# Decode attention: five of eight key pages multiplied by the query on GpSimd, summed on VectorE

## The chip, the cores and the metric

One NeuronCore of one Trainium2 chip. The metric is the device time of one execution in microseconds. All data is float32.

## The reference

One inference step of a two-layer decoder with 256 prompt tokens and 8 sample sequences of one new token each. Layer 0 is a gated MLP over positions and a mixture of experts (MoE). Then one shared key/value pair is projected. Layer 1 is block-sparse attention and a second MoE. The change lies in the attention of the 8 sample tokens. Each of these sequences has 1024 past positions, kept in 8 pages of 128 positions, which a page table scatters over a pool:

```
rows = pool[page_table]                      # keys, values: (8, 1024, 8 heads, 128)
gate = einsum('hqd,nhd->hqn', q, k_mean)     # query times the mean key of each block of 256
_, sel = top_k(gate, 3)                      # 3 of the 4 past blocks, and the own block
s = einsum('hqd,hqjkd->hqjk', q, k_g) * HEAD_DIM ** -0.5
p = softmax(concat([s, s_own]))
o = einsum('hqjk,hqjkd->hqd', p, v_g) + p_own @ v_own
```

## The kernel before

The program is written engine by engine, with semaphores by hand; each engine runs its own list in order. Keys, values and weights go through a ring of 8 slots in SBUF, filled by SyncE (SP). A page is 128 positions on 128 partitions, 1024 elements (8 heads of 128) in each; a slot holds four pages. One sequence's keys are 4 MB in 8 DMAs and its values the same. K(s) goes to slots 2-3 or 4-5, V(s) to 0-1 or 6-7, in turn. SP's order is K0, V0, K1, V1, ..., K7, V7, then the output weights and the second MoE's. K(s) waits until the scores of sequence s-2 are done (`s_made`), V(s) until the value products of s-2 are (`pv_out`); K2 waits for the V projection.

The attention loop has steps s = 0 to 8. In step s, VectorE makes the scores of sequence s and, between their pages, the softmax of sequence s-1 and the causal softmax of one prompt head (two in step 7). Scores (`keys`, L1514): TensorE spreads the query of sequence s over all partitions with matmuls against the identity (`queries`, L1119), heads 0-3 in bank 6, heads 4-7 in bank 7. VectorE runs one fused multiply and sum per page and head (L1525): key tile from SBUF times query from PSUM, summed to one score column, with the product written over the keys. It goes twice over the 8 pages, first for half 0 (heads 0-3), then for half 1. After fixed pages it does the other work:

- half 0, page 0: `blocks` (L1545), which drops the block of least score sum: L1548 to L1559, all in a chain; L1551, L1552, L1554 and the two L1557 read two SBUF operands. Page 1: `prompt_max` (L1534). Page 2: `maxima` (L1561). Page 4: `shift` (L1566, with L1570 and L1571). Page 5: `prompt_norm` (L1575, with L1578 and L1579). Page 6: `row_sums` (L1583).
- half 1, page 0: `denominators` (L1588, with L1592). Page 6: `result` (L1594).

TensorE, in step s: the prompt's logits, the transposed block maxima (L1194), their spread (L1196), the prompt's transposes, the denominator (L1203), 32 value matmuls of sequence s-1 (L1212), the prompt's values, the selection (L1221), the queries of s+1 for half 0 (`next_queries`, which waits for half 0's scores), and with the end of step s the block sums of s (L1171) and the queries of s+1 for half 1 (`open_step`). In step 0 TensorE also does the V projection (L1078), and ScalarE the copies of it (L698 to L706). ScalarE's own loop (L709) has the exponentials and the copies of PSUM banks. GpSimd has nothing in this loop: before it, it stores the k and v rows and clears a pad (L538 to L548), behind it stands the second MoE.

Of the kernel before, what the change touches and what calls it, by code (L numbers as in the profile page):

```python
# [25 lines left out]
P = 128  # L26
D = 1024
# [105 lines left out]
def program(nc, a, o):  # L133

    ctx = ExitStack()
    with ctx:
# [116 lines left out]
        dg = region(11000, H)  # L253
        hm = region(11008, 1)
        yr = region(2112, 3, D)

# [85 lines left out]
        def pair_of(name):  # L342
# [13 lines left out]

        gb_made, gcol_out, gcol_made, gD_out, sD_made, hD_made, yD_out, yD_added = (pair_of(n) for n in [
            "gb_made", "gcol_out", "gcol_made", "gD_out", "sD_made", "hD_made", "yD_out", "yD_added"])
        vecD = pair_of("vector_steps_all")
# [8 lines left out]
            "ps_out", "ps_max", "ps_exp", "ps_norm", "pT_out", "pT_made", "po_out", "po_kept"])  # L368

        qb_out, s_made, gs_out, pm_made, pm_turned, dg_made, mb_out, sc_made, se_made, rs_made, den_out = (  # L370
            sem(n) for n in ["qb_out", "s_made", "gs_out", "pm_made", "pm_turned", "dg_made", "mb_out",
# [119 lines left out]
        def _(pool):  # L491
# [45 lines left out]
            nc.gpsimd.wait_ge(rows_kept, 6)  # L537
            for rows, kname in ((krows, "k"), (vrows, "v")):  # L538
                if kname == "v":
                    pool.wait_ge(v_rows_kept, 2 * H)  # L540
                s_ = k_stored if kname == "k" else stored
                pool.dma_start(o[kname + "_prompt"][0].rearrange("(t p) h d -> p t (h d)", p=P),
                               rows[:, 0:2, :]).then_inc(s_, 16)
                pool.dma_start(o[kname + "_sample"].rearrange("b s h d -> (b s) (h d)"),
                               rows[0:NS, 2, :]).then_inc(s_, 16)
                if kname == "k":
                    pool.wait_ge(k_stored, 32)
                    nc.gpsimd.memset(pe4, 0.0).then_inc(pad_set, 1)  # L548
            moe(1)
# [3 lines left out]
        def _(act):  # L553
# [147 lines left out]
            def keep_v_rows(h):  # L701
                act.wait_ge(v_rows_out, h + 1)
                nc.scalar.activation(vrows[:, 0:2, h * HD:(h + 1) * HD],
                                     PB[2][:, 0:2 * P].rearrange("p (t d) -> p t d", t=2), ACT.Copy)\
                    .then_inc(v_rows_kept, 1)
                nc.scalar.activation(vrows[0:NS, 2, h * HD:(h + 1) * HD], PB[2][0:NS, 2 * P:3 * P], ACT.Copy)\  # L706
                    .then_inc(v_rows_kept, 1)
            act.wait_ge(pad_set, 1)
            for s in range(NS + 1):  # L709
# [21 lines left out]
                for h in V_HEADS[s]:  # L731
# [3 lines left out]
                    if h == H - 1:  # L735
                        keep_v_rows(h)
            act.wait_ge(stored, 64)
            square_and_root(3, sqM, wo_added, 0)
# [521 lines left out]
        def _(dve):  # L1260
# [253 lines left out]
            def keys(s, half, g):  # L1514

                c = s % 2
                k_slot = K_SLOT[s] + g // 4
                if g == 0:
                    dve.wait_ge(qb_out, 2 * s + half + 1)
                if g % 4 == 0 and half == 0:  # L1520
                    arrived(dve, f"K{s}", k_slot, each=64)
                for i in range(4):
                    h = 4 * half + i
                    kb = W[:, k_slot, (g % 4) * D + h * HD:(g % 4) * D + (h + 1) * HD]
                    last = v.tensor_tensor_reduce(kb, kb, PB[6 + half][:, i * P:(i + 1) * P], 1.0, 0.0,  # L1525
                                                  ALU.mult, ALU.add, sc[:, c, g, h:h + 1])
                if g == NPAGE - 1:
                    last.then_inc(s_made, 1)
# [123 lines left out]
```

## Time and profile before

| what | value |
|---|---|
| median of 3 runs | 1179.06 us |
| lowest, highest | 1178.21, 1182.37 us |
| span of the profiled execution | 1183.5 us |
| TensorE, VectorE, ScalarE, GpSimd busy | 90%, 34%, 12%, 3% |
| moved by DMA | 320.68 MB, 271 GB/s on average |
| chain that ended last | PE 82%, DVE 10% |

The profile gives the profiled execution's own time as its span, 1183.5 us. It counts from the first recorded instruction to the last, and it lies 4.4 us above the median of the timed runs. The page and the trace call TensorE PE, VectorE DVE, ScalarE ACT, GpSimd POOL and SyncE SP. A wait is given in brackets behind the instruction that ended it, with the releaser. A line number is that of the kernel.

### The profile page before, as it was taken

The page shows a single profiled execution, that of the slowest core. Times are in us where ns is not written, and L with a number is a line of the kernel's source. Part 1 is how long each engine was busy: PE and PEld are TensorE (multiplying, and loading weights), DVE is VectorE, ACT ScalarE, POOL GpSimd, SP SyncE. Part 2 cuts the span into 40 slices and gives each one's busy share as a digit, 9 for nine tenths or more (in the row PEclk, how much of TensorE's full clock was granted, in tenths as well). Part 3 has the DMA queues.
Part 4 walks back from the last instruction along what each step waited for, and adds up shares of the span by engine and source line. Part 5 has one row for each costly group of instructions (what it writes and reads, how often), then busy time and mean ns, then how long its engine had stood idle before and what let it go on. Part 6 is the DMA issues. An engine that isn't in the chain of part 4 may idle for free.

```text
span 1183.5 us, 14135 instructions
## 1 busy us (share of the span) xinstructions
PE 1068.1 (90%) x5078; PEld 686.2 (58%) x5078; DVE 408.0 (34%) x1753; ACT 145.3 (12%) x322; POOL 35.8 (3%) x56
## 2 busy tenths in 40 slices
PE   6599999989999999998999957574989999999997
PEld 4488889965455555445776734233765455554444
DVE  2034440031112121204676699987031122112113
ACT  1001001021000000002121211111121000000001
POOL 0100000010000000000000000000010000000000
PEclk9799999999999999998999967777998999999999
DMA  9802536054868998889234499999731858988881
GB/s 378 302 9 72 178 127 284 1 226 173 320 248 356 383 400 354 353 348 416 116 142 179 158 353 408 408 408 416 305 143 65 356 212 366 417 355 355 351 350 50
DMA packets 57999, 320.68 MB, mean 271 GB/s; under 512 B 6186, under 2 KB 7594, under 8 KB 47306
## 3 DMA queue, kind: packets, MB, share of 16 engines
q1 hardware_dynamic: 52880, 312.56, 66.1%
q0 software_dynamic: 1424, 5.37, 1.3%
q10 hardware_dynamic: 3634, 1.98, 0.6%
q8 instruction: 33, 0.54, 0.2%
q14 instruction: 28, 0.23, 0.1%
HBM read 315.53 MB, written 4.36 MB: 270 GB/s over the span
## 4 chain that ended last, share of the span: by engine, by line
PE 82%; DVE 10%; ACTq 3%; issue 2%; DMA 1%; SPq 1%; ACT 1%; DVEq 0%
PE bank L1013 19%; PE bank L927 11%; PE bank L1041 10%; PE bank L818 8%; PE bank L994 6%; PE bank L862 5%; PE bank L1097 5%; DVE ring L1525 4%; PE bank L1212 3%; PE bank L1250 3%; PE bank L1078 2%; PE bank L755 2%; PE bank L813 1%; DMA ring<-in_cache_k 1%; PE bank L765 1%
## 5 line engine op out<-in xcount | busy, mean ns | idle before, releaser
L1013 PE MATMUL bank<-ring,arena 128*64 128x512 f32 x1024 | 225.9, 600 | 3.2 <-DVE arena L1405 3.2
L1013 PEld LDWEIGHTS bank<-ring,arena 128*64 128x64 f32 x1024 | 76.2, 138 | 149.1 <-issue 145.6
L927 PE MATMUL bank<-arena 128*128 128x128 f32 (+1 forms) x768 | 136.6, 308 | 1.9 <-DVE xT L1454 1.9
L818 PE MATMUL bank<-arena,ring 128*128 128x264 f32 x512 | 123.4, 400 | 16.0 <-ACT arena L597 13.0
L927 PEld LDWEIGHTS bank<-arena 128*128 128x128 f32 (+1 forms) x768 | 105.1, 189 | 33.8 <-issue 5.0
L818 PEld LDWEIGHTS bank<-arena,ring 128*128 128x128 f32 x512 | 99.1, 197 | 34.4 <-ACT arena L597 13.4
L1041 PE MATMUL bank<-ring,arena 128*64 128x512 f32 x512 | 113.4, 595 | 0.3 <-issue 0.3
L1525 DVE CUSTOM_DVE_ANT_0 ring<-ring,bank 128x128 f32<-128x128 f32 x512 | 111.4, 282 | 5.2 <-DMA ring<-in_cache_k 2.2
L1460 DVE TENSOR_TENSOR arena<-arena,bank 128x512 f32<-128x512 f32 x16 | 11.0, 688 | 214.3 <-PE bank L1013 214.3
L1041 PEld LDWEIGHTS bank<-ring,arena 128*64 128x64 f32 x512 | 36.2, 137 | 63.9 <-issue 63.6
L994 PEld LDWEIGHTS bank<-arena 128*128 128x128 f32 x256 | 63.4, 333 | 15.7 <-issue 11.4
L994 PE MATMUL bank<-arena 128*128 128x264 f32 x256 | 70.3, 420 | 1.7 <-ACT arena L644 1.7
L1097 PE MATMUL bank<-arena,ring 128*128 128x264 f32 x256 | 62.8, 401 | 3.0 <-DVE arena L1279 3.0
L862 PE MATMUL bank<-arena,ring 128*128 128x264 f32 x256 | 63.5, 408 | 0.0
L862 PEld LDWEIGHTS bank<-arena,ring 128*128 128x128 f32 x256 | 61.7, 334 | 2.2 <-DVE xT L1343 2.2
L1454 DVE TENSOR_TENSOR xT<-xT,bank 128x264 f32<-128x264 f32 x128 | 55.0, 429 | 13.0 <-PE bank L994 7.8
L1405 DVE COPY arena<-bank 128x512 f32<-128x512 f32 x16 | 11.1, 692 | 137.0 <-PE bank L927 137.0
L1097 PEld LDWEIGHTS bank<-arena,ring 128*128 128x128 f32 x256 | 49.4, 197 | 14.0 <-DVE arena L1279 3.4
L1212 PE MATMUL bank<-ring,arena 128*32 128x512 f32 x256 | 43.2, 835 | 0.0
L1473 DVE COPY arena<-bank 128x512 f32<-128x512 f32 x16 | 11.1, 692 | 90.1 <-PE bank L1041 90.1
L1525 DVE DVE_READ_ACCUMULATOR2_ANT arena<- 128x1 f32 x512 | 41.8, 82 | 0.0
L1492 DVE RECIPROCAL arena<-arena 128x264 f32<-128x264 f32 x16 | 28.8, 1803 | 24.9 <-ACT arena L670 24.9
(205 smaller groups left out, 856.2 us busy)
## 6 DMA issues: line engine op xcount, KB each, us to landing
ring<-in_moe_w_gate SPq DMA_DIRECT2D x32, 2048.0 KB, 16.8
ring<-in_moe_w_up SPq DMA_DIRECT2D x32, 2048.0 KB, 14.7
ring<-in_moe_w_down SPq DMA_DIRECT2D x32, 2048.0 KB, 12.5
ring<-in_cache_k SPq DMA_DIRECT2D x64, 512.0 KB, 7.5
ring<-in_cache_v SPq DMA_DIRECT2D x64, 512.0 KB, 6.0
ring<-in_a_w_in SPq DMA_DIRECT2D x8, 2048.0 KB, 26.2
ring<-in_a_w_out SPq DMA_DIRECT2D x4, 2048.0 KB, 8.0
ring<-in_w_kv SPq DMA_DIRECT2D x4, 2048.0 KB, 24.1
```

The source lines that it names most:

```text
L818: return mm(bank[:, 0:T], slot(base + k // 2, 2)[:, k % 2, j * P:(j + 1) * P], hT[:, k, :], start=(k == 0), stop=(k == KT - 1))
L862: last = mm(PB[j % 2][:, 0:T], slot(c // 4, 4)[:, c % 4, j:D:KT], vT[:, c, :], start=(c == 0), stop=(c == CT - 1))
L927: last = mm(PB[k // 4][:, (k % 4) * P:(k % 4 + 1) * P], hr[0:n, t, k * P:(k + 1) * P], hot[0:n, t, :, :].rearrange("p e s -> p (e s)"), st ...
L994: last = mm(y_bank(i, j)[:, 0:T], dr[:, j:D:KT], sT, start=True, stop=True)
L1013: last = mm(bank[64 * e:64 * e + 64, :], hg[:, k, CAP * e:CAP * (e + 1)], slot(base + e, KT)[:, k, :], start=(k == 0), stop=(k == KT - 1))
L1041: last = mm(PB[4 + half][64 * e:64 * e + 64, :], heT[:, f, CAP * e:CAP * (e + 1)], slot(down[0] + e, FT)[:, f, 512 * half:512 * (half + 1) ...
L1097: last = mm(acc(g)[:, 0:T], w, h[:, k, :], start=(k == 0), stop=(k == KT - 1))
L1212: last = mm(PB[4][32 * q:32 * q + 32, :], pe4[:, c, g, :], W[:, v_slot + g // 4, (g % 4) * D + 512 * half:(g % 4) * D + 512 * (half + 1)], ...
L1250: last = mm(PB[j % 2][:, 0:T], slot(W_O + h // 4, 4)[:, h % 4, j:D:KT], aT[:, h, :], start=(h == 0), stop=(h == H - 1))
L1454: v.tensor_tensor(xT[:, j, :], xT[:, j, :], y_bank(i, j)[:, 0:T], ALU.add).then_inc(moe_done if isinstance(i, int) and i == NPAIR - 1 else ...
L1492: link(v.reciprocal(rsh, rmh))
L1525: last = v.tensor_tensor_reduce(kb, kb, PB[6 + half][:, i * P:(i + 1) * P], 1.0, 0.0, ALU.mult, ALU.add, sc[:, c, g, h:h + 1])
```

## The change

For sequences 1 to 7, pages 1, 2, 4, 5 and 7 are multiplied on GpSimd, a whole page of 1024 elements for all heads at once, in place. VectorE sums each such page over 128 elements for 8 heads with one reduction in half 1. Pages 0, 3 and 6 stay as they were, and sequence 0 too. As GpSimd reads its query from SBUF, ScalarE copies the two banks into a new tile `qrow`, of two buffers. `qrow` lies where the normed input of the K and V projections lay, so the first copy waits for the V projection to end. VectorE's first page of a half waits for the copy instead of the matmuls. The first half's `s_made` is given after page 6. The stores of the rows are written as a function, and four pairs of semaphore names in the MoE are shared by two forms of it of which one runs.

```
+        qrow = region(0, 2, D)
+        BY_POOL = (1, 2, 4, 5, 7)
...
-        gb_made, gcol_out, gcol_made, gD_out, sD_made, hD_made, yD_out, yD_added = (pair_of(n) for n in [
-            "gb_made", "gcol_out", "gcol_made", "gD_out", "sD_made", "hD_made", "yD_out", "yD_added"])
+        sD_made, hD_made, yD_out, yD_added = silu_made, he_made, y_out, y_added
+        gcol_out, gcol_made, gD_out, gb_made = sT_out, sT_made, heT_out, heT_made
...
+        q_kept, k_by_pool = sem("q_kept"), sem("k_by_pool")
...
+            store_rows(krows, "k", k_stored)
+            pool.wait_ge(k_stored, 32)
+            nc.gpsimd.memset(pe4, 0.0).then_inc(pad_set, 1)
+            pool.wait_ge(v_rows_kept, 2 * H)
+            store_rows(vrows, "v", stored)
+            for s in range(1, NS):
+                pool.wait_ge(q_kept, 2 * s)
+                for g in BY_POOL:
+                    arrived(pool, f"K{s}", K_SLOT[s] + g // 4, each=64)
+                    kb = W[:, K_SLOT[s] + g // 4, (g % 4) * D:(g % 4 + 1) * D]
+                    nc.gpsimd.tensor_tensor(kb, kb, qrow[:, s % 2, :], ALU.mult).then_inc(k_by_pool, 1)
             moe(1)
...
+            def keep_q(s, half):
+
+                act.wait_ge(qb_out, 2 * s + half + 1)
+                if s == 1 and half == 0:
+                    act.wait_ge(vp_out, H)
+                nc.scalar.activation(qrow[:, s % 2, 512 * half:512 * (half + 1)], PB[6 + half][:, :], ACT.Copy)\
+                    .then_inc(q_kept, 1)
...
+                if s + 1 < NS:
+                    keep_q(s + 1, 0)
+                    keep_q(s + 1, 1)
             act.wait_ge(stored, 64)
...
+                by_pool = s >= 1 and g in BY_POOL
                 if g == 0:
-                    dve.wait_ge(qb_out, 2 * s + half + 1)
-                if g % 4 == 0 and half == 0:
+                    if s == 0:
+                        dve.wait_ge(qb_out, half + 1)
+                    else:
+                        dve.wait_ge(q_kept, 2 * (s - 1) + half + 1)
+                if half == 0 and g % 4 == 0:
                     arrived(dve, f"K{s}", k_slot, each=64)
...
+                if by_pool and half == 1:
+                    dve.wait_ge(k_by_pool, (s - 1) * len(BY_POOL) + BY_POOL.index(g) + 1)
+                    last = v.tensor_reduce(sc[:, c, g, :], W[:, k_slot, (g % 4) * D:(g % 4 + 1) * D]
+                                           .rearrange("p (h d) -> p h d", h=H), AX.X, ALU.add)
+                elif not by_pool:
+                    for i in range(4):
+                        h = 4 * half + i
+                        kb = W[:, k_slot, (g % 4) * D + h * HD:(g % 4) * D + (h + 1) * HD]
+                        last = v.tensor_tensor_reduce(kb, kb, PB[6 + half][:, i * P:(i + 1) * P], 1.0, 0.0,
+                                                      ALU.mult, ALU.add, sc[:, c, g, h:h + 1])
+                if g == (6 if s >= 1 and half == 0 else NPAGE - 1):
                     last.then_inc(s_made, 1)
```

## Rows read from the trace of the kernel before

**Rows 1.** The page's 40 slices of 29.6 us: busy tenths of VectorE and DMA engines.
```profile
DVE  2034440031112121204676699987031122112113
...
DMA  9802536054868998889234499999731858988881
```

**Rows 2.** Windows: length, busy us by engine, granted TensorE clock, DMA share, GB/s.
```profile
720.45:740.90 20.45, 12.78 (x74) 7.00 (x74) 18.69 (x154) 2.72 (x8) 0.00 (x0) 0.75 1.03 407
820.00:825.00 5.00, 2.52 (x9) 1.91 (x9) 3.35 (x26) 0.88 (x2) 0.00 (x0) 0.61 1.02 433
```

**Rows 3.** The chain of waits around the keys of sequence 7: start, us, what.
```profile
788.04 12.11 DMA ring<-in_cache_k
```

**Rows 4.** VectorE's timeline: ends of sequence 1's, 6's and 7's scores, start of 7's.
```profile
695.74 0.08 DVE L1525 DVE_READ_ACCUMULATOR2_ANT arena<- 128x1 f32 x1
...
798.19 0.08 DVE L1525 DVE_READ_ACCUMULATOR2_ANT arena<- 128x1 f32 x1
800.29 0.29 DVE L1525 CUSTOM_DVE_ANT_0 ring<-ring,bank 128x128 f32<-128x128 f32 x1 [2.03 <-DMA ring<-in_cache_k]
...
821.96 0.08 DVE L1525 DVE_READ_ACCUMULATOR2_ANT arena<- 128x1 f32 x1
```

**Rows 5.** VectorE's timeline in one step, which begins at 736.74.
```profile
736.66 0.08 DVE L1525 DVE_READ_ACCUMULATOR2_ANT arena<- 128x1 f32 x1
...
737.17 0.28 DVE L1525 CUSTOM_DVE_ANT_0 ring<-ring,bank 128x128 f32<-128x128 f32 x1
...
737.38 0.28 DVE L1525 CUSTOM_DVE_ANT_0 ring<-ring,bank 128x128 f32<-128x128 f32 x1
...
740.92 0.29 DVE L1539 TENSOR_REDUCE arena<-arena 128x1 f32<-128x128 f32 x1
741.13 0.41 DVE L1540 TENSOR_REDUCE arena<-arena 128x1 f32<-128x256 f32 x1
...
746.31 0.29 DVE L1578 TENSOR_SCALAR arena<-arena 128x128 f32<-128x128 f32 x1
746.51 0.35 DVE L1579 TENSOR_SCALAR arena<-arena 128x256 f32<-128x256 f32 x1
...
747.89 0.25 DVE L1585 TENSOR_REDUCE arena<-arena 128x8 f32<-128x64 f32 x1
...
756.22 0.17 DVE L1596 TENSOR_TENSOR arena<-arena,bank 128x8 f32<-128x8 f32 x1 [0.90 <-PE bank L1221]
```

**Rows 6.** Groups of GpSimd's products by shape: busy us, mean ns, idle before.
```profile
L516 POOL TENSOR_TENSOR arena<-arena,roots 128x264 f32<-128x264 f32 x16 | 11.3, 736 | 289.0 <-DVE roots L1275 289.0
...
L499 POOL TENSOR_TENSOR wr<-arena,gains 128x128 f32<-128x128 f32 x2 | 0.8, 403 | 0.0
...
L499 POOL TENSOR_TENSOR wr<-arena,gains 128x32 f32<-128x32 f32 x2 | 0.5, 243 | 2.3 <-DMA arena<-in_moe_w_re 2.3
```

**Rows 7.** Timelines of ScalarE and TensorE: a 128x512 copy, a half's query matmuls.
```profile
734.01 0.60 ACT L725 ACTIVATE arena<-bank 128x512 f32<-128x512 f32 x1 [6.07 <-PE bank L1212]
...
737.07 1.11 PE L1122 MATMUL bank<-consts,arena 128*128 128x128 f32 x8
```

**Rows 8.** Timelines in the second MoE, where GpSimd multiplies from 879.07 to 884.72.
```profile
880.49 0.73 POOL L516 TENSOR_TENSOR arena<-arena,roots 128x264 f32<-128x264 f32 x1
...
879.93 0.20 DVE L1353 TENSOR_TENSOR arena<-bank,rbias 128x40 f32<-128x40 f32 x1 [0.41 <-PE bank L895]
...
880.64 0.61 DVE L1367 TENSOR_TENSOR arena<-arena,consts 128x12 f32<-128x12 f32 x1
...
881.98 0.67 DVE L1371 TENSOR_TENSOR arena<-arena 128x12 f32<-128x12 f32 x1
...
883.43 0.20 DVE L1377 TENSOR_REDUCE arena<-arena 128x12 f32<-128x48 f32 x1
```

**Rows 9.** Step 1: ScalarE's last copy of V rows, GpSimd's last row store.
```profile
678.62 0.25 ACT L706 ACTIVATE arena<-bank 8x128 f32<-8x128 f32 x1
...
679.92 0.52 POOL L544 DMA_DIRECT2D out_v_sample<-arena  x1
```

More of the change, by code:

```diff
@@ L537, in _, with store_rows @@
             nc.gpsimd.wait_ge(rows_kept, 6)
[L538 to L541, printed above, removed]
+            def store_rows(rows, kname, done):
                 pool.dma_start(o[kname + "_prompt"][0].rearrange("(t p) h d -> p t (h d)", p=P),
-                               rows[:, 0:2, :]).then_inc(s_, 16)
+                               rows[:, 0:2, :]).then_inc(done, 16)
                 pool.dma_start(o[kname + "_sample"].rearrange("b s h d -> (b s) (h d)"),
[L545 to L548, printed above, removed]
+                               rows[0:NS, 2, :]).then_inc(done, 16)
+            store_rows(krows, "k", k_stored)
[9 more added lines that the diff above has]
+                    nc.gpsimd.tensor_tensor(kb, kb, qrow[:, s % 2, :], ALU.mult).then_inc(k_by_pool, 1)
             moe(1)
@@ L1517, in keys @@
                 k_slot = K_SLOT[s] + g // 4
+                by_pool = s >= 1 and g in BY_POOL
                 if g == 0:
-                    dve.wait_ge(qb_out, 2 * s + half + 1)
-                if g % 4 == 0 and half == 0:
-                    arrived(dve, f"K{s}", k_slot, each=64)
[L1522 to L1527, printed above, removed]
+                    if s == 0:
[3 more added lines that the diff above has]
+                if half == 0 and g % 4 == 0:
+                    arrived(dve, f"K{s}", k_slot, each=64)
+                if by_pool and half == 1:
[9 more added lines that the diff above has]
+                if g == (6 if s >= 1 and half == 0 else NPAGE - 1):
                     last.then_inc(s_made, 1)
```

## The prediction

> **What bounds the kernel now.** I read the slices of the page first. In the decode-attention stage, about 697 to 822 us, VectorE shows 9, 9, 9, 8, 7 tenths and the DMA engines 9 throughout [rows 1]. So two resources are full side by side, and the question is which lets go last. The windows say it more finely: a stretch of 20.45 us holds 18.69 us of VectorE instructions and no GpSimd work, at a DMA share of 1.03 and 407 GB/s [rows 2]. One step moves the keys and values of one sequence: 16 pages of 0.524 MB, 8.39 MB; at 0.408 MB per us that is 20.5 us, the step's own length. In the chain of waits the keys' DMA ends a piece of 12.11 us at 800.15 [rows 3], and VectorE starts sequence 7 at 800.29 after 2.03 us of waiting for it [rows 4]. VectorE paces the stage up to there by a hair, the transfer paces its last step. Behind the last score at 822.04 [rows 4] comes a fixed sequence of round trips, the output projection and the second MoE, which move 1:1 with it.
>
> In a step, 64 fused products at a pitch of 0.21 us (737.17 to 737.38 [rows 5]) are 13.3 us; the small instructions and one wait are the other 7.1 us. The change attacks the 13.3 us, but the transfer stays 20.5 us a step. That caps what it can bring: an earlier VectorE waits for K7 at 800.29, and only the 21.75 us from there to 822.04 can shrink.
>
> **VectorE, added and removed.** In sequences 1 to 7, 40 of 64 products go: 40 x 0.208 = 8.3 us. Five sums over 128x1024 come. The trace has none; reductions of 128 and 256 elements take 0.29 and 0.41 us [rows 5], so 0.96 ns an element and 0.41 + 768 x 0.96 ns = 1.15 us, 1.06 us as pitch (an instruction begins 0.08 us before the end printed for the one before). Bounds: 0.98 us (1024 x 0.96 ns) and 1.64 us (four times the 256 row). I take 1.06: five are 5.3 us, net 3.0 us less per step. But cover goes too. From the row sums' start to the result lie 8.33 us (747.89 to 756.22, with a wait of 0.90 for TensorE [rows 5]): denominator, 32 value matmuls, a copy, a selection, none of them shortened. VectorE would then have 0.17+0.83+0.50+2.12+0.83+2.12+0.83 = 7.4 us in it and wait 0.9 us, as now. Undisturbed, a step is 7.85 us to its row sums (today 747.89 - 736.74 = 11.15, less 16 products), 8.33, and 1.14 for result and last sum: 17.3 us. Under the transfer's 20.5, so that would decide.
>
> **GpSimd.** 35 products of 128x1024, both operands in SBUF. Rows: 128x32 0.243 us, 128x128 0.403 us, 128x264 0.735 us [rows 6]. First to third, the slope is 0.492 us/232 = 2.12 ns an element: 2.35 us, 2.31 as pitch. Low end 1.9 us (the slope between the first two, 1.67 ns), high end 2.85 us (the 264 row in proportion). I take 2.31, since that row alone has two full operands. Five are 11.6 us, below a step, so GpSimd is not itself the bound. It starts once both halves of the query are in SBUF: the last score of a step ends at 736.74 [rows 5], the four query matmuls' end at 738.18, ScalarE's 128x512 copy takes 0.60 us [rows 7]. That is 2.2 us into the step; the products end at 4.5, 6.8, 9.1, 11.5 and 13.8. The 14 copies on ScalarE are 8.4 us on an engine busy 2.72 of 20.45 us [rows 2]; behind them it next waits for maxima, so they cost nothing outside step 1. If GpSimd's queue were late, behind it stands only the second MoE's first work.
>
> **Two engines in one another's way.** The trace already shows GpSimd and VectorE meeting. While GpSimd multiplies 128x264 at a pitch of 0.70 us (one starts at 880.49, so the next at 881.19), VectorE's L1367, 12 elements with two SBUF operands, starts at 880.64 and takes 0.61 us, to 881.25; L1371 starts at 881.98 and takes 0.67 us, to 882.65, where product ends fall at 881.89 and 882.59. A reduction in between takes 0.20 us, and an add with a PSUM operand 0.20 us [rows 8]. So: a VectorE instruction with two SBUF operands is held to the end of the running GpSimd product; one with a single SBUF operand is not, which frees the key products (their query is in PSUM) and the sums. The Trainium skill, SBUF — State Buffer, section Who interferes with whom, states that rule: the pair excludes each other for the whole instruction. The trace agrees, with 0.61 us for what takes 0.17. The same section counts a two-port fp32 tensor_scalar among the held; no row here has one beside GpSimd, and by it case 2 below (1187) would fall away.
>
> Two SBUF operands have, in a step: L1551, L1552, L1554 and twice L1557 (block choice), L1570 and L1571 (shift), L1592. L1578 and L1579 have one, but 128 elements more cost them 0.06 us [rows 5], 2.1 elements a ns against the reductions' 1.04: they must use a second way in. I count them held; unheld is case 2. An instruction issued unlinked behind a held one (L1571, L1557's second) I let slip through with it; that it loses another 2.3 us is case 3. An ordinary step, from its last score: the block choice reaches L1557 at 2.3, just as GpSimd starts, and ends at 2.8. Causal maxima 1.3, block maxima 0.6, page 3 0.83, the add before L1570 0.2: 5.6. L1570 held to 6.9, L1578 to 9.2, L1579 to 11.6. Page 6; row sums at 12.5. Result at 20.8, last page's sum done at 21.96. Today 798.27 - 695.84 = 102.43 us for five steps [rows 4], 20.49 each. 5 x 1.47 = +7.4 us.
>
> **Step 1.** VectorE now waits there for the copied query, and ScalarE makes it only after its last V rows (678.87 [rows 9]): halves at 679.5 and 680.1. Today page 0 and the block choice are done earlier, in the shadow of the V projection. They now stand behind 679.5 and meet GpSimd at once, whose row stores leave it at 680.44 [rows 9]: products end at 682.8, 685.1, 687.4, 689.7, 692.1. L1551, L1552, L1554, L1557 are held to the first, second, third, fourth. Row sums at 695.4, the step ends at 704.9; today it ended at 695.84 [rows 4], with row sums 9.3 us before, 686.6. +9.0 us.
>
> **The queue of SP.** V2 waits for the values of sequence 0, so it starts 8.8 us later and K3 and all pages with it. K7 lands at 809.1 instead of 800.3, and is wanted at 704.9 + 109.8 = 814.7: hidden. **Step 7** has two heads: 1.4 us more, 23.4 us, against 822.04 - 798.27 = 23.8 with its wait. -0.4. Sum: 9.0 + 7.4 - 0.4 = +16.0 us on the profiled execution's 1183.5 us. That execution is 4.4 us (0.4%) above the median of the runs; the difference is carried over whole: 1179.1 + 16.0 = 1195.1.
>
> The other edits cost nothing: semaphore names shared by two forms of the MoE of which one runs; row stores in the old order on the old queue; the first half's semaphore at page 6, which frees the query's bank sooner.
>
> **The rivals.** (1) Not slower: the holds don't bite, say because GpSimd's reads of wide tiles leave gaps. Then 17.3 us of work stand in 20.5 us of transfer. Row sums of step 1 come 0.8 us later (687.4), K7 too; the last step takes 17.3 + 1.4 = 18.7 us instead of 21.75: -2.2, 1176.9. It decides from the point where a step's holds are below 3 us. Against it: [rows 8]. 0.17. With pages at the 433 GB/s of 820 to 825 us [rows 2], 99 us of transfer would be 5.7 us shorter still: 1171; nothing says pages get that. 0.06. (2) L1578 and L1579 not held: steps of 18.7 us, so the transfer decides, 8.8 us late: 8.8 + 20.95 - 21.75 = +8.0, 1187. 0.17. (3) Every unlinked second instruction is held again, and the tiny L1543 and L1564: steps of 25.3 us, step 1 +11.3, step 7 26.7: 11.3 + 24.2 + 2.9 = +38, 1217. 0.12. The forecast runs from +5 (products of 1.9 us) to +32 (2.85 us), 1184 to 1211; sums of 1.64 us would add about 14. 0.48.
>
> **The numbers.** 1195 us. The range 1177 to 1211 takes in case 2 and the forecast and touches case 1. A measurement of this kernel tells 0.5%, 6 us, from no change: faster 0.06, same 0.20 (case 1 and the low edge of the forecast), slower 0.74.
>
> **What would show it.** Right: five GpSimd products of about 2.3 us a step; L1570 and L1578 of 1 to 2 us instead of 0.17 and 0.29; L1551 to L1557 long in step 1 alone; steps near 22 us; DMA share below 1 from step 3 on; sequence 1's first key product at 679.5. Wrong: L1578 still 0.29 us (case 2); steps of 20.5 us with VectorE waiting for keys (case 1); a page's sum far from 1.15 us; GpSimd products above 3.4 us, since then 2.2 + 5 x 3.4 + 1.1 = 20.3 us and GpSimd itself is the bound; key products longer than 0.28 us.

## The result, and the profile after

| what | before | after |
|---|---|---|
| median, lowest to highest, us | 1179.02, 1178.21 to 1182.37 | 1232.59, 1231.50 to 1240.36 |
| span of the profiled execution, us | 1183.5 | 1229.8 |
| VectorE, GpSimd busy | 34%, 3% | 37%, 9% |

The changed kernel is slower: ratio 1.0456, 95% interval 1.0418 to 1.0494, +53.6 us. The forecast was 1195 us; the measured time lies above the range's high end of 1211 us. The direction and the kind of cause were right; which instructions pay, and so the size, was not.

The two profiled executions don't start the attention stage at the same time: the first key product of sequence 0 is at 651.69 us before and at 645.64 us after, so the difference of the spans (46.3 us) understates what the stage lost. A profiled execution's span lies 1.7 us under its time here (1229.8 and 1231.50 us), so that of before took some 1185 us, about 6 us above the median, and its stage begins 6.05 us later. Below, the stage is measured from that product to the first instruction of the last block choice: 171.58 us before, 223.09 us after, +51.5 us. That is nearly all of the loss.

The 40 slices of the page (30.7 us each), as [rows 1]: busy tenths of VectorE and the DMA engines.

```profile
DVE  2024440040111210146665999999304012121013
DMA  9702544067698888894345588888903769888881
```

In slices 24 to 28 (707 to 861 us) VectorE shows 9 as before, but the DMA engines no longer do: 8 instead of 9. One step of the stage, from the end of sequence 1's scores at 702.70 to that of sequence 2's, in the columns of [rows 2]:

```profile
702.70:729.95 27.25, 13.60 (x74) 7.15 (x74) 24.81 (x80) 3.93 (x11) 11.54 (x5) 0.69 0.84 311
```

The step takes 27.25 us where [rows 2] had 20.45. VectorE has 80 instructions instead of 154 and is nevertheless busy for 24.81 us instead of 18.69. The transfer ran at 407 GB/s there and runs at 311 here, share 0.84 instead of 1.03: it now waits for VectorE, since the ring's slots come free later (the share is 1.00 and more up to 723 us, and 0.01 from 724 to 726). GpSimd works 11.54 us. From sequence 1's end on the step hardly varies: from one block choice to the next the seven steps take 29.72, 27.23, 27.27, 27.37, 27.26, 27.28 and 28.43 us, where they took 28.29, 20.45, 20.47, 20.47, 20.68, 22.39 and 22.14 before.

Where it goes is in the timelines of this step, GpSimd's first and then VectorE's. The line numbers have moved: L1580, L1581, L1583 and L1586 are the L1551, L1552, L1554 and L1557 of before, L1572 is L1543, L1593 is L1564, L1599 and L1600 are L1570 and L1571, L1607 and L1608 are L1578 and L1579, L1614 the row sums (L1585), L1625 the result (L1596), L1554 the fused product (L1525), which is not the L1554 of before, now L1583. An `x5` in a timeline row is five instructions without a gap, and its second number is their whole length.

```profile
704.86 11.54 POOL L558 TENSOR_TENSOR ring<-ring,arena 128x1024 f32<-128x1024 f32 x5 [18.94 <-ACT arena L723]
```

```profile
703.05 0.29 DVE L1554 CUSTOM_DVE_ANT_0 ring<-ring,bank 128x128 f32<-128x128 f32 x1 [0.33 <-ACT arena L723]
...
704.61 0.19 DVE L1581 TENSOR_TENSOR arena<-arena,consts 128x32 f32<-128x32 f32 x1
...
705.07 2.18 DVE L1583 TENSOR_TENSOR arena<-arena 128x32 f32<-128x32 f32 x1
707.28 4.56 DVE L1586 SCALAR_TENSOR_TENSOR arena<-arena 128x32 f32<-128x32 f32 x2
...
713.29 0.83 DVE L1572 TENSOR_SCALAR arena<-arena 128x2 f32<-128x2 f32 x1
...
714.35 2.08 DVE L1593 TENSOR_SCALAR arena<-consts,arena 8x8 f32<-8x8 f32 x1
...
717.38 0.17 DVE L1599 TENSOR_TENSOR arena<-arena 128x8 f32<-128x8 f32 x1
...
718.04 0.29 DVE L1607 TENSOR_SCALAR arena<-arena 128x128 f32<-128x128 f32 x1
...
719.62 0.26 DVE L1614 TENSOR_REDUCE arena<-arena 128x8 f32<-128x64 f32 x1
...
728.66 0.17 DVE L1625 TENSOR_TENSOR arena<-arena,bank 128x8 f32<-128x8 f32 x1 [1.27 <-PE bank L1241]
728.74 1.21 DVE L1548 TENSOR_REDUCE arena<-ring 128x8 f32<-128x1024 f32 x1
```

Five products at a pitch of 2.30 us from 704.86 end at 707.20, 709.50, 711.81, 714.11 and 716.40. Now look at the ends of the long rows of VectorE: L1583 at 707.25, the two L1586 together at 711.84 (two product ends), L1572 at 714.12, L1593 at 716.43. Each held instruction gives way to one product, VectorE does the unheld work behind it, and the next one runs into the next product. So five products meet exactly five instructions. L1581 comes just before GpSimd starts and takes its 0.19 us; L1599 and L1607 come after the last product and are as short as ever. Unheld, the five would be 0.87 us (0.19, 0.29, 0.17 and 0.22: the first experiment); they print 9.65.

Step 1 looks different. GpSimd, then VectorE:

```profile
673.87 0.52 POOL L546 DMA_DIRECT2D out_v_sample<-arena  x1
674.40 11.52 POOL L558 TENSOR_TENSOR ring<-ring,arena 128x1024 f32<-128x1024 f32 x5
```

```profile
674.67 11.30 DVE L1580 TENSOR_TENSOR arena<-arena 128x32 f32<-128x32 f32 x1
```

One single instruction of 128x32 elements is held for 11.30 us, over all five products (674.40 + 11.52 = 685.92). Behind it nothing is left to meet, and the row sums follow at 692.45.

### The profile page after: what moved, and what is told of

Read it like the earlier page. It is cut to its first block, busy times and chain, and to the rows that moved or that the text cites. A ratio compares the mean times of both kernels' runs of the same rounds, so it can differ in the third digit from the quotient of the medians.

```text
span 1229.8 us, 13674 instructions
## 1 busy us (share of the span) xinstructions
PE 1070.6 (87%) x5078; PEld 685.0 (56%) x5078; DVE 453.0 (37%) x1228; ACT 153.5 (12%) x336; POOL 116.5 (9%) x91
## 4 chain that ended last, share of the span: by engine, by line
PE 80%; DVE 14%; ACTq 2%; issue 1%; ACT 1%; DMA 0%; DVEq 0%; SPq 0%
PE bank L1033 18%; PE bank L947 11%; PE bank L1061 9%; PE bank L838 8%; PE bank L1014 6%; PE bank L882 5%; PE bank L1117 5%; PE bank L1232 4%; PE bank L1270 3%; DVE arena L1586 2%; PE bank L1098 2%; PE bank L775 2%; DVE ring L1554 1%; PE bank L833 1%; DVE arena L1583 1%
## 5 line engine op out<-in xcount | busy, mean ns | idle before, releaser
L1033 PE MATMUL bank<-ring,arena 128*64 128x512 f32 x1024 | 222.5, 592 | 2.5 <-DVE arena L1425 2.5
L1061 PE MATMUL bank<-ring,arena 128*64 128x512 f32 x512 | 113.4, 595 | 0.3 <-issue 0.3
L558 POOL TENSOR_TENSOR ring<-ring,arena 128x1024 f32<-128x1024 f32 x35 | 80.7, 2340 | 97.7 <-ACT arena L723 97.7
L1425 DVE COPY arena<-bank 128x512 f32<-128x512 f32 x16 | 11.1, 692 | 137.0 <-PE bank L947 137.0
L533 POOL TENSOR_TENSOR arena<-arena 128x384 f32<-128x384 f32 x16 | 13.3, 831 | 485.6 <-PE bank L1050 468.7
L1554 DVE CUSTOM_DVE_ANT_0 ring<-ring,bank 128x128 f32<-128x128 f32 x232 | 51.4, 281 | 17.9 <-ACT arena L723 16.3
L1214 PE MATMUL bank<-consts,arena 128*8 128x128 f32 x8 | 3.0, 376 | 60.9 <-DVE arena L1588 60.9
L1232 PE MATMUL bank<-ring,arena 128*32 128x512 f32 x256 | 49.2, 939 | 0.0
## 6 DMA issues: line engine op xcount, KB each, us to landing
ring<-in_a_w_in SPq DMA_DIRECT2D x8, 2048.0 KB, 26.6
```

The costliest lines, as they stand in the source:

```text
L558: nc.gpsimd.tensor_tensor(kb, kb, qrow[:, s % 2, :], ALU.mult).then_inc(k_by_pool, 1)
L1033: last = mm(bank[64 * e:64 * e + 64, :], hg[:, k, CAP * e:CAP * (e + 1)], slot(base + e, KT)[:, k, :], start=(k == 0), stop=(k == KT - 1))
L1061: last = mm(PB[4 + half][64 * e:64 * e + 64, :], heT[:, f, CAP * e:CAP * (e + 1)], slot(down[0] + e, FT)[:, f, 512 * half:512 * (half + 1) ...
L1232: last = mm(PB[4][32 * q:32 * q + 32, :], pe4[:, c, g, :], W[:, v_slot + g // 4, (g % 4) * D + 512 * half:(g % 4) * D + 512 * (half + 1)], ...
```

## The experiments

Two theories to begin with. Theory A: the loss is VectorE's instructions that need the path to SBUF it shares with GpSimd, each held to the end of the running product, and any two-operand or tensor_scalar instruction counts. Rival B: the loss is in the order that the change brings, with the query's way over ScalarE, the later first page and the thinner cover for TensorE's round trips. Where not said otherwise, each edit is to the changed kernel, and times stand beside runs of the kernel before on the same chip.

| run | median us | ratio to before, 95% | block choice to block choice, us |
|---|---|---|---|
| e1_no_products | 1177.54 | 0.9988, 0.9962 to 1.0014 | 17.85, 17.51, 20.42, 21.41, 21.42, 20.46, 19.24 |
| e2_from2 | 1222.09 | 1.0342, 1.0307 to 1.0376 | 28.91, 26.96, 27.10, 27.16, 27.23, 27.32, 28.49 |
| e3_late | 1195.54 | 1.0117, 1.0049 to 1.0186 | 21.22, 22.16 (five times), 25.18 |
| e4_memset | 1177.98 | 0.9993, 0.9959 to 1.0026 | 19.67, 20.33, 20.40, 20.51, 20.42, 20.46, 20.38 |
| e5_one_page | 1204.03 | 1.0194, 1.0165 to 1.0224 | 23.34, 23.63, 23.77, 23.83, 23.85, 23.88, 23.74 |
| e6_halves | 1223.56 | 1.0360, 1.0301 to 1.0418 | 30.11, 24.71, 26.00, 24.95, 26.13, 25.01, 27.08 |
| e7_store_late | 1229.95 (one) | | 27.20, 26.76, 27.02, 27.24, 27.20, 27.26, 28.45 |
| e8_probe | 1248.17 (one) | | none: a measurement behind the kernel's end |
| e9_late3 | 1179.59 | 0.9998, 0.9981 to 1.0015 | 29.30, 20.10, 20.30, 18.93, 20.95, 21.42, 23.39 |

**Without the products.** GpSimd only counts its semaphore up, so the sums run over unmultiplied keys.

```
-                    nc.gpsimd.tensor_tensor(kb, kb, qrow[:, s % 2, :], ALU.mult).then_inc(k_by_pool, 1)
+                    pool.sem_inc(k_by_pool, 1)
```

> Left out: GpSimd's 35 products (it only counts the semaphore up), so the sums run over unmultiplied keys; copies, waits and sums stay. Theory H, holds: VectorE's instructions of 32 elements no longer wait for GpSimd's products. L1583 falls from 2.17 to 0.19 us, the two L1586 from 4.56 to 0.29 together, L1572 from 0.83 to 0.17, L1593 from 2.08 to 0.22, and L1580 of step 1 from 11.3 to 0.19. Steps of 27.25 us lose at least 8 us and come to the 20.5 us of the transfer; total 1177 us. Rival L, lost cover: the 40 products that are gone covered round trips to TensorE and ScalarE, and the copied query comes late; then steps stay at 25 to 27 us and the total at 1220 to 1232 us. Rival S, the sums cost more than their 1.13 us: as L.

Measured: no difference from the kernel before. The query's copies, the sums and the order are all still there, so rival B falls as the cause of the loss: where the transfer sets the step, what they cost is hidden. Every hold is gone; the same instructions in step 1:

```profile
674.65 0.19 DVE L1583 TENSOR_TENSOR arena<-arena 128x32 f32<-128x32 f32 x1
674.88 0.29 DVE L1586 SCALAR_TENSOR_TENSOR arena<-arena 128x32 f32<-128x32 f32 x2
...
676.62 0.17 DVE L1572 TENSOR_SCALAR arena<-arena 128x2 f32<-128x2 f32 x1
...
677.00 0.22 DVE L1593 TENSOR_SCALAR arena<-consts,arena 8x8 f32<-8x8 f32 x1
```

It also shows why there was nothing to win. Freed of 8.3 us of fused products a step and given five sums, VectorE needs 17.34 us in step 2 from score end to score end; from one block choice to the next it is 17.51 us, 0.51 us of waiting for the next keys included. From there on it has caught up with the transfer. VectorE's waits between 650 and 830 us (in all, how often, the longest), and 60 us of the stage in the columns of [rows 2]:

```profile
DVE ring L1554 <- DMA ring<-in_cache_k: 14.9, 5, 4.5
```

```profile
720.00:780.00 60.00, 34.77 (x210) 20.21 (x206) 44.80 (x229) 11.74 (x30) 0.00 (x0) 0.75 1.03 409
```

VectorE is busy 44.80 of 60 us, the DMA share is 1.03 as before. The products themselves, in the changed kernel, cost 1232.6 - 1177.5 = 55 us.

**GpSimd from sequence 2 on.** Sequence 1 is done as before the change; the indices of the semaphores follow.

```
-            for s in range(1, NS):
-                pool.wait_ge(q_kept, 2 * s)
+            for s in range(2, NS):
+                pool.wait_ge(q_kept, 2 * (s - 1))
...
-                by_pool = s >= 1 and g in BY_POOL
+                by_pool = s >= 2 and g in BY_POOL
```

> Sequence 1 as before the change (all on VectorE from PSUM); GpSimd from sequence 2. Theory H: step 1 ends again as before the change, which takes back 12.9 us (step 1 ended 12.9 us later than before once the stages are laid over one another): 1219 to 1220 us. The other steps stay 27.2 us. A question beside it: in step 1 of the changed kernel one instruction was held over all five products (11.30 us), in all later steps to the end of one. If that comes from being the first products behind GpSimd's own row stores, no such long hold shows now; if the first meeting of the stage is always so long, it shows in step 2, and the total is 9 us higher. Rival L expects the same 12.9 us, so this run only sizes a term.

Measured 1222.09 us, 10.5 us less than the changed kernel, where 12.9 were expected. From the first key product to the second block choice it is 45.61 us, where the changed kernel has 58.25 and the one before 44.98: step 1 gives its 12.6 us back, and the stage as a whole 13.2 (209.87 us). But this execution enters the stage 3.0 us later, which the edit doesn't touch. Step 1 was thus worth a fifth to a quarter of the loss. The other steps stay at 27 us. The first burst is now in step 2, and it does not hold one instruction for all of it:

```profile
694.94 2.34 DVE L1579 TENSOR_TENSOR arena<-arena,consts 128x32 f32<-128x32 f32 x1
...
697.56 2.03 DVE L1581 TENSOR_TENSOR arena<-arena 128x32 f32<-128x32 f32 x1
699.62 4.56 DVE L1584 SCALAR_TENSOR_TENSOR arena<-arena 128x32 f32<-128x32 f32 x2
```

So the 11.30 us are not a matter of the first burst as such. What else stands only in step 1 of the changed kernel are GpSimd's row stores directly ahead of it; that is the seventh experiment.

**The products behind the small instructions.** GpSimd waits for the row sums too, and so starts when block choice, maxima and normalizing are done.

```
                 pool.wait_ge(q_kept, 2 * s)
+                pool.wait_ge(rs_made, s)
```

> GpSimd's products of a step wait until VectorE has issued the row sums of that step; all five pages as in the change. Theory H: the small chain of half 0 runs undisturbed, row sums 8.5 us into the step; the products fill the next 11.6 us, the last sum ends near 21.5 us, only L1621 can be held. Steps of 21.5 us, step 1 ends 4.6 us later than before the change: 1179 + 4.6 + 5 + 0.5 = 1189 us, although GpSimd's work starts 6 us later in each step. Rival S, GpSimd's own length is what the step waits for: starting it 6.3 us later makes steps 6.3 us longer, 33 us, total 1270 us. Rival L: no change of the steps, 1230 us.

Measured 1195.54 us (1192.41 and 1198.67): 37 us of the loss are gone with the same products in the same number, though 6.5 fewer than expected. One held instruction is left in an ordinary step, and the steps end with GpSimd:

```profile
707.58 1.34 DVE L1622 TENSOR_TENSOR arena<-arena 128x8 f32<-128x8 f32 x1
...
717.85 0.17 DVE L1626 TENSOR_TENSOR arena<-arena,bank 128x8 f32<-128x8 f32 x1
718.19 1.22 DVE L1549 TENSOR_REDUCE arena<-ring 128x8 f32<-128x1024 f32 x1 [0.18 <-POOL ring L559]
```

The burst starts 9.3 us into the step (at 706.53) and takes 11.62, the last sum takes the rest: 22.16 us. The result is there at 717.85 and is no longer what is late. This is 1.7 us a step above the transfer's 20.45 [rows 2]: five products are too many to start that late. The expectation had 21.5 us; and in step 7 (25.18 us) a tensor_scalar of the second prompt head is held for 2.25 us besides.

**Fills instead of products.** As many instructions of GpSimd on the same tiles, that only write.

```
-                    nc.gpsimd.tensor_tensor(kb, kb, qrow[:, s % 2, :], ALU.mult).then_inc(k_by_pool, 1)
+                    nc.gpsimd.memset(kb, 0.5).then_inc(k_by_pool, 1)
```

> In place of GpSimd's products GpSimd fills the same five pages with a constant: it writes the same 128x1024 tiles and reads nothing; results are then not those of the reference. A fill should take 1.0 to 1.1 us a page. Theory H with the clash on the read side: no holds, 1177 us as without products. Theory H with the clash on the write side too: L1583 and its followers are held for up to 1.0 us each, five fills, steps of at most 21.5 us, total 1178 to 1190 us and holds of 0.4 to 1.0 us in the rows. Rival L: 1220 to 1232 us.

Measured: no difference from the kernel before. The rows of a line give its least, median and greatest duration in ns over all its instructions; first those of the changed kernel, then those with fills:

```profile
L1572 DVE TENSOR_SCALAR arena<-arena x8: 169/830/841, 688.4 to 861.6; 128x2 f32<-128x2 f32 x8
L1583 DVE TENSOR_TENSOR arena<-arena x8: 192/2172/2176, 686.5 to 869.9; 128x32 f32<-128x32 f32 x8
```

```profile
L1572 DVE TENSOR_SCALAR arena<-arena x8: 169/2337/2343, 677.3 to 809.3; 128x2 f32<-128x2 f32 x8
L1583 DVE TENSOR_TENSOR arena<-arena x8: 191/191/193, 675.4 to 817.5; 128x32 f32<-128x32 f32 x8
```

Beside fills the two-operand L1583 runs free (191 ns, at most 193; in step 2 it starts at 695.03, in the fills that run from 694.79 to 699.31), and of the rows here only the tensor_scalar of 128x2 elements is held: 2337 ns, to the end of the last of the five fills, which take 4.52 us together. GpSimd's being busy is thus not what holds L1583; its reading of SBUF is. The tensor_scalar is held by either. Step lengths stay at the transfer's 20.4 us: 17.5 us of work and 2.2 of holding fit under it.

**One page a step.** Does the number of products or the fact of one set the price?

```
-        BY_POOL = (1, 2, 4, 5, 7)
+        BY_POOL = (7,)
```

> GpSimd multiplies only page 7 of sequences 1 to 7; the other seven pages stay fused on VectorE. Theory H, one GpSimd product holds one VectorE instruction for what is left of it: of a step's small instructions only L1583 is held (about 2 us), L1586, L1572 and L1593 fall back to 0.2 us. Row sums 13.4 us into the step, steps of 23.0 us, step 1 ends 6 us later than before the change: 1179 + 6 + 13 + 1 = 1199 us. Rival P, the loss is in proportion to GpSimd's work: a fifth of 53 us, 1190 us. Rival L, the loss is in the lost cover: hardly any cover is lost, 1180 to 1183 us.

Measured 1204.03 us, 5 us above the 1199 expected and far from both rivals. One product a step (2.34 us from 725.13), one held instruction a step:

```profile
725.34 2.17 DVE L1583 TENSOR_TENSOR arena<-arena 128x32 f32<-128x32 f32 x1
...
745.45 0.17 DVE L1625 TENSOR_TENSOR arena<-arena,bank 128x8 f32<-128x8 f32 x1 [2.41 <-PE bank L1241]
```

The step is 23.8 us, where 23.0 were expected: 11.15 us to the row sums as before [rows 5], 2.0 of hold and 0.33 of query are 13.5; from row sums to result it takes 9.0 (736.44 to 745.45) instead of 8.33, with the last sum 1.3. That 0.7 us a step is what the 5 us come from, and it lies in TensorE's value matmuls (see the account of the prediction below). Of the page's 1.7 us of fused products that VectorE saves here behind the row sums nothing is won: it waits 2.41 us for TensorE instead of 0.90. The held time is then lost whole.

**Half as long products, twice as many.**

```
-                    nc.gpsimd.tensor_tensor(kb, kb, qrow[:, s % 2, :], ALU.mult).then_inc(k_by_pool, 1)
+                    for part in range(2):
+                        nc.gpsimd.tensor_tensor(kb[:, 512 * part:512 * (part + 1)], kb[:, 512 * part:512 * (part + 1)],
+                                                qrow[:, s % 2, 512 * part:512 * (part + 1)], ALU.mult).then_inc(k_by_pool, 1)
```

> Each product of GpSimd is cut into two of 512 elements (ten a step, about 1.25 us each, 12.5 us in all instead of 11.5). Theory H: every held instruction waits for one product of 1.25 us, so the first holds get shorter and more instructions are held (L1599, L1600, L1607 and L1608 too); row sums at 15.9 us instead of 16.9, steps 1.0 us shorter, 1225 us. Rival B, VectorE waits until GpSimd's whole burst is over, however it is cut: the burst is 1 us longer, steps 28 us, 1238 us.

Measured 1223.56 us, where theory A had 1225. The holds are about half as long (L1585 is L1583, 1.09 us instead of 2.18) and there are more of them:

```profile
708.65 1.09 DVE L1585 TENSOR_TENSOR arena<-arena 128x32 f32<-128x32 f32 x1
...
716.97 1.35 DVE L1602 TENSOR_TENSOR arena<-arena 128x64 f32<-128x64 f32 x1
...
718.69 0.86 DVE L1609 TENSOR_SCALAR arena<-arena 128x128 f32<-128x128 f32 x1
719.47 1.36 DVE L1610 TENSOR_SCALAR arena<-arena 128x256 f32<-128x256 f32 x1
```

Here the two instructions that the prediction had counted as held (L1578 and L1579, now L1609 and L1610) do meet products, and are held. In the changed kernel they only came too late for it. The burst sets the price as long as VectorE has something that can be held: in step 1 one instruction takes 12.02 us again, beside ten products now. The steps alternate between 25 and 26 us though the holds are the same. The difference is again in the value matmuls: in steps 2 to 6 their 32 take 5.19, 6.48, 5.43, 6.60 and 5.49 us, at a mean granted clock of 0.69, 0.56, 0.66, 0.54 and 0.66.

**The row stores behind sequence 1's products.**

```
-            pool.wait_ge(v_rows_kept, 2 * H)
-            store_rows(vrows, "v", stored)
             for s in range(1, NS):
+                if s == 2:
+                    pool.wait_ge(v_rows_kept, 2 * H)
+                    store_rows(vrows, "v", stored)
                 pool.wait_ge(q_kept, 2 * s)
```

> GpSimd's stores of the value rows are issued after the products of sequence 1 instead of before. A question on one row: L1580 was held for 11.30 us in step 1, over five products, where later steps have one product to a hold. If GpSimd's row stores, issued just ahead, are the cause, L1580 is now held to the end of the first product only and L1581, L1583 and both L1586 to the next ends; the block choice then ends at the last product as before or up to 1 us earlier, so the time stays within 2 us of 1232. If the cause is another, L1580 keeps its 11 us.

The first burst, now without stores issued ahead of it (GpSimd from 673.98 for 11.52 us):

```profile
674.79 1.58 DVE L1581 TENSOR_TENSOR arena<-arena 128x32 f32<-128x32 f32 x1
676.40 2.27 DVE L1582 TENSOR_TENSOR arena<-arena,consts 128x32 f32<-128x32 f32 x1
...
681.00 4.56 DVE L1587 SCALAR_TENSOR_TENSOR arena<-arena 128x32 f32<-128x32 f32 x2
```

The 11.30 us have become one product's rest (L1581 is the L1580 of the changed kernel), and five instructions are held again, L1584 between these rows among them (2.02 us). So the hold over the whole burst goes with the row stores issued just ahead of it. They don't do it alone: ahead of the fills of e4_memset they stand too, and there the same instruction takes 0.19 us. Step 1 is 2.5 us shorter; the time, a single run of 1229.95 us, is not to be told from the changed kernel's (1231.50 to 1240.36). Whether one instruction waits for five products or five for one each, most of the burst is sat out.

**Single instructions beside a burst.** At the end of the kernel before, 24 products of 128x1024 run on GpSimd without a gap, and VectorE issues one instruction at every second product's start; then twelve fills of 0.95 us. The work is additional to the kernel's own.

```
+            for i in range(24):
+                nc.gpsimd.tensor_tensor(page(i), page(i), W[:, 7, 0:D], ALU.mult).then_inc(pr_p, 1)
+            pool.wait_ge(pr_d, 1)
+            for i in range(12):
+                nc.gpsimd.memset(page(i), 0.5).then_inc(pr_m, 1)
...
+            for i, kind in enumerate(kinds):
+                dve.wait_ge(pr_p, 2 * i + 1)
+                kind()
```

> The kernel before, with a stretch added behind its last copies: 24 GpSimd products of 128x1024 back to back, beside them one VectorE instruction of each kind, started as a product begins and waited for; then 12 GpSimd fills of 128x1024 with four of the kinds. Theory H: held to the end of a product (2.1 to 2.3 us instead of 0.2): the multiply of 8 elements with two SBUF operands, each of an unlinked pair in its turn (over 4 us for both), the tensor_scalar of 8 elements and the copy of 256 from SBUF to SBUF. Not held: the sum of 1024 (1.2 us), the multiply and the fused product with PSUM, the tensor_scalar from PSUM. A question is tensor_scalar of 7 elements and the reciprocal. The multiply of 1024 with two SBUF operands is held 2.2 us and then runs its 1.2, and puts the next product back by about 1.2 us. Beside fills: the two-operand multiply is free, the tensor_scalar of 8 and the copy are held. Rival: only the number of SBUF operands counts, then tensor_scalar and copy are free in both parts. The time is some 75 us over the kernel before.

VectorE's timeline, products first, then (from 1234.99) fills, and the products' own least, median and greatest duration:

```profile
1184.74 2.29 DVE L1646 TENSOR_TENSOR ring<-ring 128x8 f32<-128x8 f32 x2 [2.38 <-POOL ring L557]
1189.35 2.21 DVE L1653 TENSOR_SCALAR ring<-ring 128x8 f32<-128x8 f32 x1 [2.32 <-POOL ring L557]
1193.93 2.22 DVE L1654 TENSOR_SCALAR ring<-ring 128x7 f32<-128x7 f32 x1 [2.38 <-POOL ring L557]
1198.52 2.35 DVE L1655 COPY ring<-ring 128x256 f32<-128x256 f32 x1 [2.37 <-POOL ring L557]
1203.16 1.22 DVE L1656 TENSOR_REDUCE ring<-ring 128x8 f32<-128x1024 f32 x1 [2.29 <-POOL ring L557]
1207.77 0.42 DVE L1657 TENSOR_TENSOR ring<-bank,ring 128x256 f32<-128x256 f32 x1 [3.38 <-POOL ring L557]
...
1216.95 0.20 DVE L1660 RECIPROCAL ring<-ring 128x8 f32<-128x8 f32 x1 [4.26 <-POOL ring L557]
...
1226.14 3.28 DVE L1646 TENSOR_TENSOR ring<-ring 128x1024 f32<-128x1024 f32 x1 [4.03 <-POOL ring L557]
1234.99 0.17 DVE L1646 TENSOR_TENSOR ring<-ring 128x8 f32<-128x8 f32 x1 [5.58 <-POOL ring L560]
1237.74 0.81 DVE L1653 TENSOR_SCALAR ring<-ring 128x8 f32<-128x8 f32 x1 [2.58 <-POOL ring L560]
```

```profile
L557 POOL TENSOR_TENSOR ring<-ring x24: 2332/2337/3319, 1177.7 to 1231.6; 128x1024 f32<-128x1024 f32 x24
```

Held by products: two SBUF operands, tensor_scalar even with 7 elements, copy. Not held: a reduction, a PSUM operand (the tensor_scalar from PSUM, not shown, takes 0.17 us), reciprocal. The `x2` row is the pair issued unlinked: both within 2.29 us and not the 4 us expected, so the second of 8 elements slips through, as the prediction assumed; the second L1586, of 32 elements, and L1602 above, of 64, did not. By fills only tensor_scalar and copy are held. And a long VectorE instruction with two operands strikes back: 3.28 us, with one product at 3.32 instead of 2.34.

The Trainium skill, SBUF — State Buffer, section Who interferes with whom, counts tensor_scalar with two ports among what is held, and says that two SBUF inputs meet GpSimd's reads but not its writes. These runs agree with both: 2.21 and 0.81 us, and 2.29 against 0.17 us.

**The version that the results point to.** GpSimd from sequence 2 on, behind the row sums, and three pages (4, 5, 7) only, so that its burst ends in time.

```
-        BY_POOL = (1, 2, 4, 5, 7)
+        BY_POOL = (4, 5, 7)
...
-            for s in range(1, NS):
-                pool.wait_ge(q_kept, 2 * s)
+            for s in range(2, NS):
+                pool.wait_ge(q_kept, 2 * (s - 1))
+                pool.wait_ge(rs_made, s)
```

> A version meant to keep clear of the holds: sequence 1 as before the change; from sequence 2 on GpSimd multiplies three pages (4, 5, 7), and only after the row sums of the step. Theory H: no instruction of half 0 is held, L1622 of half 1 for at most 1.4 us; VectorE's step is 19.8 us by its rows, under the 20.5 us in which the pages arrive, so the transfer sets the steps and at most the last step gains: 1175 to 1181 us, not to be told from the kernel before. If VectorE's time were the bound in the kernel before, steps would fall to 19.8 us and the time by 4 us or more, to 1175 us or less. Rival L, lost cover costs by itself: slower, 1190 us or more.

Measured over five rounds: ratio 0.9998, 0.9981 to 1.0015. No difference from the kernel before, and no version beat it.

```profile
720.00:780.00 60.00, 38.57 (x222) 21.07 (x222) 54.58 (x327) 11.70 (x30) 21.07 (x9) 0.76 1.03 408
```

VectorE is busy 54.58 of 60 us, one 1.35 us hold a step included, the transfer is full at 1.03 and 408 GB/s, and VectorE waits for keys (4.2 us in two waits between 650 and 830 us). That is the ceiling of [rows 2], reached again from the other side.

## Why the prediction was wrong in size

**Right: what bounds the stage, and that nothing was to be won.** The prediction put an undisturbed step at 17.3 us of work under 20.5 us of transfer and the time without holds at 1176.9 us. The first experiment has 17.34 us and 1177.5 us.

**Right: GpSimd.** Product 2.35 us at a pitch of 2.31 forecast, 2.34 at 2.30 measured; start 2.2 us into the step forecast, 2.16 measured (702.70 to 704.86). **Right: step 1's start.** First key product at 679.5 forecast; 673.3 measured, on a stage that began 6.05 us earlier, so 679.4.

**Right: that holds make it slower, and the rule for two operands.** Wrong was the tally of an ordinary step: 21.96 us forecast from score end to score end, 27.25 measured. Line numbers in this account are those of the kernel before. The 5.3 us:

- *Which instructions are held, and so how far the burst reaches: +4.1.* The step that failed is "An instruction issued unlinked behind a held one (L1571, L1557's second) I let slip through with it", together with the count that left L1543 and L1564 out. The second L1557 is held again, and both tiny tensor_scalars are held. And the very first, L1554, was placed a hair ahead of GpSimd's start and came 0.21 us behind it (705.07 and 704.86), by less than the 0.33 us of the next point. The forecast had three holds, on L1570, L1578 and L1579, 4.65 us in all, two product ends of the five falling where VectorE did free work. Measured are five holds in a row, 8.78 us. L1570, L1578 and L1579 were never met, since VectorE reached them 1 us after the burst's end. And holds chain: the fuller the list is of such instructions, the nearer VectorE comes to sitting out the whole burst (start 2.16, five pitches of 2.30, 13.7 us in all, and the row sums 3.2 us later).
- *The query: +0.33.* TensorE spreads a new query's first half only after the selection, so the step starts with a wait for ScalarE's copy, [0.33 <-ACT arena L723]. The prediction took the second half's way and not the first's, and said that the copies cost nothing outside step 1. Row sums are 16.9 us into the step, where the forecast had 12.5.
- *Row sums to result: +0.7.* 9.04 us (719.62 to 728.66), 8.33 forecast. The prediction held this way constant ("none of them shortened") and gave no term to TensorE's clock. The 32 value matmuls in it, from the first's start to the last's end, in the columns of [rows 2]: the kernel before, the changed kernel, the first experiment, one page a step.

```profile
748.73:754.41 5.68, 5.68 (x34) 1.31 (x33) 5.61 (x56) 0.00 (x0) 0.00 (x0) 0.64 1.03 406
```

```profile
720.45:726.84 6.39, 6.39 (x34) 1.46 (x33) 6.32 (x22) 0.00 (x0) 0.00 (x0) 0.56 0.54 209
```

```profile
699.07:704.36 5.29, 5.29 (x34) 1.22 (x33) 5.22 (x19) 0.00 (x0) 0.00 (x0) 0.68 1.03 413
```

```profile
737.28:743.64 6.36, 6.36 (x34) 1.47 (x33) 5.69 (x55) 0.00 (x0) 0.00 (x0) 0.57 1.03 410
```

Length times granted clock is 3.6 us in all four, so the lengths differ by the clock, a mixture of its two levels, 1.2 and 2.4 GHz. The lost cover is not the reason: the first experiment has the same cover gone, and the way takes 7.94 us there in step 2 and VectorE waits 0.17 us; with one page on GpSimd nearly all the cover is there, and it takes 9.0. In the changed kernel the clock is at its lower level from 709 to 726 us, after TensorE had 0.01 us of matmuls from 704.80 to 709.00 and waited 7.39 us for the held block choice and then 3.90 for the held maxima; before, the two waits were 0.81 and 3.14 us. A held VectorE thus costs more than the hold: 27.25 us against the 17.34 of the step without products are 8.8 us of holds and 1.1 us of slower value matmuls.

- *The last sum: +0.15.* 1.21 us, nothing following it, and not the 1.06 of the pitch.

Steps 2 to 6 sum to 136.4 us where 109.8 were forecast, +26.6. Step 1 adds 3.9 (its end is 708.8 us counted as in the trace of before, 704.9 forecast: all five products were sat out and not four, and the way to the result was longer here too) and step 7 5.0 (28.4 for 23.4). The +16.0 forecast and these 35.5 are the 51.5 us of the stage. The prediction's case 3, "every unlinked second instruction is held again, and the tiny L1543 and L1564", had steps of 25.3 us and 1217 us with a chance of 0.12. It was the nearest: with the 1.2 us of the last three points it comes to 26.5 of the 27.25 us, and in the rest, 0.75 us, lies that L1554 meets the burst already. It stood outside the range, because the prediction let the second of an unlinked pair slip through without a row that shows one: L1367 and L1371 [rows 8] are not such a pair. For the tiny tensor_scalars L1543 and L1564 it gave no reason, though it counted the wide ones, L1578 and L1579, as held.

**Open.** Why one instruction is held over the whole burst when row stores were issued just ahead (11.30 us, 12.02 with halves): the runs show that it goes with the stores, not how. Nor does a run tell why beside fills one tensor_scalar is held to the end of the burst, and why TensorE's clock alternates from step to step with the half products.

## What to carry to other kernels

Moving wide work from VectorE to GpSimd is not free for the small instructions that stay: each with two SBUF operands, and each tensor_scalar and copy from SBUF to SBUF, that meets a GpSimd instruction reading SBUF waits for its end, and a chain of them waits for nearly the whole burst. TensorE waits along, and may come back at its lower clock, as it did here. Before such a move, see what the freed engine runs into next (here the transfer, at a share of 1.03), since that caps the gain at the difference; and if the move is made, put the burst where VectorE has reductions and PSUM operands to do, not where its small instructions stand. In a forecast, an instruction that slips through a hold needs a row that shows one slipping.

## What the runs showed of the hardware that was not expected

- A hold of 11.30 us on 128x32 elements, five products long, with software-issued row stores directly ahead of the burst; 1.58 us with the stores moved behind it.
- Beside five fills without a gap a tensor_scalar of 128x2 waited 2.34 us, over more than one fill (0.95 us each), while two-operand instructions took their 0.19 us.
- A tensor_scalar of 128x7 elements is held as one of 128x8 is (2.22 and 2.21 us), a reciprocal of 128x8 is not (0.20 us).
- The same 32 value matmuls took 5.19 to 6.60 us, depending on TensorE's granted clock in them (0.69 and 0.54 at the two ends).
- A second unlinked instruction of 8 elements slipped through with the first; of 32 and 64 elements it was held anew.
- GpSimd pays too: its product took 3.32 instead of 2.34 us beside a two-operand VectorE instruction of 128x1024.
